# Routing a 64-expert layer: expert slots from eight rounds of max8 instead of ranks and one-hot matmuls, all gate/up products as split float32r passes, and the sum kept in two tensors

## The reference

```python
scores = sigmoid(t @ w_router)                  # 512 tokens x 64 experts, f32
sel = scores + b_router
# the best 4 of 8 groups (sum of each group's top 2), then the top 8 experts within them
w = scores at the 8 experts; w = w / w.sum() * 2.5
y = (silu(t @ w_sh_gate) * (t @ w_sh_up)) @ w_sh_down            # shared expert
y += sum over e: w[:, e] * ((silu(t @ w_gate[e]) * (t @ w_up[e])) @ w_down[e])
x = x + y
x = x + sigmoid(rms_norm(x) @ w_ple_gate) * rms_norm(p @ w_ple_proj)
```

## Time and profile before

| | |
|---|---|
| three runs | 1226.49, 1230.92, 1232.58 us (median 1230.92) |
| the profiled execution | 1230.64 us, of which 1228.9 us span |
| busy: PE, DVE, ACT, POOL | 1170.2, 811.1, 716.4, 311.3 us |
| expert loop, from the silu of expert 1 to that of 63 | 534.04 to 1152.29 us |
| mean granted clock of TensorE | 0.984 |

### The profile page before, as it was taken

One profiled execution on the slowest core, in us unless ns is written; L12 is line 12 of the kernel. 1 busy time (PEld: TensorE's weight loads), 2 busy tenths in 40 slices (PEclk: granted clock), 3 DMA queues, 4 the chain that ended last, 5 costly groups with the idle time before them and its releaser, 6 DMA issues. The chain is left out here.

```text
span 1228.9 us, 17964 instructions
## 1 busy us (share of the span) xinstructions
PE 1170.2 (95%) x5557; PEld 891.3 (73%) x5557; DVE 811.1 (66%) x1351; ACT 716.4 (58%) x1263; POOL 311.3 (25%) x291
## 2 busy tenths in 40 slices
PE   5999999998999999799999999999999999999778
PEld 5988888686566874377777777777777777777566
DVE  6336442387343426488888888888888888888642
ACT  5534442375343242277777777777777777777651
POOL 1210000051364000123233333333333333333200
PEclk9999999999899999899999999999999999999979
DMA  6313212024002068379999999999999999999641
GB/s 226 138 69 106 99 68 88 20 73 171 1 1 86 25 249 312 150 247 360 358 368 375 367 372 378 368 366 363 357 367 368 362 365 374 370 374 328 171 156 52
DMA packets 71756, 290.34 MB, mean 236 GB/s; under 512 B 15107, under 2 KB 20262, under 8 KB 46758
## 3 DMA queue, kind: packets, MB, share of 16 engines
q1 hardware_dynamic: 51846, 252.05, 53.2%
q0 software_dynamic: 19296, 35.71, 11.7%
q10 hardware_dynamic: 576, 2.10, 0.4%
HBM read 282.45 MB, written 41.94 MB: 264 GB/s over the span
## 5 line engine op out<-in xcount | busy, mean ns | idle before, releaser
L636 POOL DMA_INDIRECT moe_sum<-ya,sidx x64 | 132.1, 2064 | 397.7 <-DMA moe_sum<-ya,sidx 345.4
L1358 DVE TENSOR_TENSOR arena_r<-arena,win_r 128x1024 fp32r<-128x1024 f32 x192 | 223.2, 1218 | 0.5 <-ACT win_r L902 0.4
L902 ACT ACTIVATE win_r<-arena 128x1024 fp32r<-128x1024 f32 x192 | 191.3, 1094 | 10.7 <-PE bank L1657 10.7
L1738 PE MATMUL bank<-win_r,work_r 128*128 128x512 f32 x384 | 176.6, 460 | 0.0
L1376 DVE TENSOR_TENSOR arena_r<-arena,hT_r 128x1024 fp32r<-128x1024 f32 x128 | 151.2, 1222 | 29.7 <-ACT hT_r L921 29.7
L1740 PE MATMUL bank<-arena_r,work_r 128*128 128x512 f32 x384 | 150.0, 391 | 0.0
L1739 PE MATMUL bank<-win_r 128*128 128x512 f32 x384 | 149.7, 390 | 0.0
L921 ACT ACTIVATE hT_r<-arena 128x1024 fp32r<-128x1024 f32 x128 | 129.1, 1070 | 0.0
L1730 PE MATMUL bank<-arena,work 128*128 128x512 f32 x256 | 122.3, 601 | 1.6 <-ACT work L912 1.6
L1492 PE MATMUL bank<-arena_r,hT_r 128*128 128x512 f32 (+2 forms) x320 | 120.8, 378 | 0.1
L1496 PE MATMUL bank<-win_r,hT_r 128*128 128x512 f32 (+2 forms) x320 | 120.6, 377 | 0.0
(11 more groups left out here) (268 smaller groups left out, 2142.7 us busy)
## 6 DMA issues: line engine op xcount, KB each, us to landing
arena<-in_w_exp_gate SPq DMA_DIRECT2D x64, 1024.0 KB, 8.2
arena<-in_w_exp_up SPq DMA_DIRECT2D x64, 1024.0 KB, 11.6
arena<-in_w_exp_down SPq DMA_DIRECT2D x64, 1024.0 KB, 6.6
win<-in_w_in SPq DMA_DIRECT2D x8, 2048.0 KB, 7.8
win<-in_w_o SPq DMA_DIRECT2D x2, 2048.0 KB, 7.6
arena<-in_w_ple_gate SPq DMA_DIRECT2D x2, 2048.0 KB, 11.1
win<-in_mla_w_qb SPq DMA_DIRECT2D x4, 576.0 KB, 4.0
resid<-in_x SPq DMA_DIRECT2D x4, 512.0 KB, 5.0
```

Source lines behind the costliest of these rows:

```text
L636: pool.indirect_dma_start(sum_dram, bass.IndirectOffsetOnAxis(sidx[j % 2][0:NS, 0:1], 0), yo[j % 2][0:NS], None, bounds_check=last_token, ...
L902: act.activation(gu_hi[n % 2][:, :, cols], gu_w[n % RING][:, :, cols], ACT.Copy).then_inc(gu_hi_r, 1)
L1358: dve.tensor_tensor(gu_lo[n % RING][:, :, cols], gu_w[n % RING][:, :, cols], gu_hi[n % 2][:, :, cols].bitcast(F32), ALU.subtract).then_inc ...
L1738: pe.matmul(b_, x_hi[:, k, :], w_hi, start=False, stop=False)
```

## The change

- **Slots.** The key of a token for an expert is 4096 minus its number where the expert was chosen, else 0 (`rt_K`). PE transposes the keys once, so that 128 partitions hold 64 experts x two halves of the tokens, 256 keys each. Eight rounds of `max` (the 8 largest) and `match_replace` (strike them out) list the tokens of every half: 64 slots for each half of each expert (`tops_of`). Two copies and one matmul put the lists into slot order (`lists_of`, `slots_T`), and one instruction turns all keys into token numbers `idx`, 128 slots x 64 experts (`slot_tokens`). `one_hot`, `tab`, `tokens_of`, the ranks, the table `R` and `iota` go. An expert now fits in one pass if neither half of the tokens has more than 64 for it. In the last two steps of the loop the eight rounds run once more, for a next pass.
- **Weights.** The 64 combine weights of a token are stored behind its row, so a gathered row has 1088 instead of 1024 values. POOL copies column D + j of the gathered rows to `wt` for `hidden`, and column j of `idx` to the index tiles of gather and scatter: three copies of 128 x 1 for an expert.
- **Gate/up.** `KS` goes: all 8 blocks are split. There are four instead of three pieces of 128 x 1024 on ACT and on DVE, two instead of three copies of the transposed rows on ACT, and 24 split passes instead of 18 plus the 4 direct records.
- **Two sums.** Even experts are added to `sums[0]`, which starts as x (stored early), odd ones to `sums[1]`, which starts as the shared expert's output. A scatter waits only for the one two before it. After the loop both are loaded and DVE adds them (`add_odd`).
- **Shared expert.** Its steps are reordered: PE banks 0 to 3 for gate/up, and banks 6/7, 0/1, 2/3, 6/7 for the four outputs, copied (not added) by ACT for tiles 0 and 1 and by DVE for tiles 2 and 3. `sh_hidden(0)` stands behind the routing on DVE. Its weights use the other window buffer. The first half of the high parts of down now stands ahead of the silu on ACT. The zeroing of the gathered rows' buffers goes.

```diff
-        KS = 6
-        NPR = KS // 2
+        NPR = KD // 2
...
             def scatter(b, q, j):
-                pool.wait_ge(yA, at(b, q, 2, 2 * (j + 1)))
-                pool.wait_ge(yB, at(b, q, 1, j + 1))
                 if q is None and j == 0:
                     pool.wait_ge(sum_st, 16 * NT)
+                elif q is None and j == 1:
+                    pool.wait_ge(sum_odd_st, 16 * NT)
                 else:
-                    pool.wait_ge(scat[(j - 1) % 2], at(b, q, 8, 16 * ((j - 1) // 2 + 1)))
+                    pool.wait_ge(scat[j % 2], at(b, q, 8, 16 * (j // 2)))
                 pool.sem_inc(held, 1)
-                pool.indirect_dma_start(sum_dram, bass.IndirectOffsetOnAxis(sidx[j % 2][0:NS, 0:1], 0),
+                pool.tensor_copy(sidx[j % 2][:, :], tokens(q, j)).then_inc(sidx_set, 1)
+                pool.wait_ge(sidx_set, at(b, q, 1, j + 1))
...
+                pool.wait_ge(y_out, at(b, q, 2, 2 * (j + 1)))
+                pool.sem_inc(held, 1)
+                pool.indirect_dma_start(sums[j % 2], bass.IndirectOffsetOnAxis(sidx[j % 2][0:NS, 0:1], 0),
...
             def step(b, q, j):
                 if q is not None or 1 <= j <= E:
                     scatter(b, q, j - 1)
+                if q is not None or 0 <= j + 1 < E:
+                    weight(b, q, j + 1)
                 if q is not None or j + 3 < E:
                     gather(b, q, j + 3)
...
+            def tops_of(b, rounds):
+                for i in rounds:
+                    best = tops_[:, 8 * i:8 * i + 8]
+                    for c in range(2):
+                        ins = (dve.max(best, keys_) if c == 0 else
+                               dve.match_replace(out=keys_, in_to_replace=best, in_values=keys_, imm_value=0.0))
+                        ins.then_inc(tops_step, 1)
+                        n = 2 * i + c + 1
+                        dve.wait_ge(tops_step, n if b is None else at(b, None, 2 * ROUNDS / E, 2 * ROUNDS + n))
...
             def step(b, q, j):
                 free = q is None
-                if not free or j + 3 < E:
-                    select(b, q, j + 3)
...
                     b_ = bank[2 + j % 2][:, :]
-                    for k in range(KS, KD):
-                        pe.matmul(b_, x_f[:, k - KS, :], wgu[j % RING][:, k], start=(k == KS), stop=False)
                     pe.wait_ge(xt_hi, at(b, q, 2, 2 * j + 2))
-                    pe.wait_ge(xtb, at(b, q, 1, j + 1))
-                    for k in range(KS):
+                    pe.wait_ge(xt_lo, at(b, q, 1, j + 1))
+                    for k in range(KD):
...
+            sh_gate_up(0)
...
+            pe.wait_ge(K_ready, 1)
+            for c in range(2):
+                pe.transpose(KT[:, c * P:(c + 1) * P], rt_K[:, 2 * c:2 * c + 2, :].rearrange("q t e -> q (t e)"), ident[:, :])
...
+            sh_gate_up(1)
+            sh_gate_up(2)
+            slots_T(None)
+            sh_hidden_T(0)
+            sh_gate_up(3)
+            sh_hidden_T(1)
...
+            sh_down(0, 6)
+            sh_hidden_T(2)
+            sh_down(1, 0)
+            sh_hidden_T(3)
+            sh_down(2, 2)
+            pe.wait_ge(sh_y_act, 1)
+            sh_down(3, 6)
```

More of the change, by code:

```diff
@@ L82, in sem @@
             return ctx.enter_context(nc.semaphore(name))
+        bank = [ctx.enter_context(nc.psum_tensor(f"bank{i}", [P, 512], F32)) for i in range(8)]
         def v2(t, at, x, y):
@@ L211, in hybrid_block_kernel @@
         sidx = [sb(f"sidx{i}", 1, U32) for i in range(2)]
-        slots = [sm[:, 180 + 2 * i:182 + 2 * i] for i in range(4)]
-        wt = [z[:, 1:2] for z in slots]
+        wt = [sm[:, 180 + i:181 + i] for i in range(4)]
         rows = sb("rows", P)
@@ L249, in hybrid_block_kernel @@
         cmp_ = work[:, 964:964 + NPASS_MAX]
-        addt = sm[:, 176:180]
-        pcol = sm[:, 192:193]
-        bank = [ctx.enter_context(nc.psum_tensor(f"bank{i}", [P, 512], F32)) for i in range(8)]
+        kcol = sm[:, 176:180]
+        KT, counts, slot_keys = bank[5][:, 0:2 * P], bank[5][:, 2 * P:3 * P], bank[5][:, 0:E]
         ld_x = [sem(f"x_loaded{t}") for t in range(NT)]
@@ L443, in _ @@
             expert_dn(1, 1)
+            for t in range(NT):
+                sp.wait_ge(h2_n, t + 1)
+                sp.dma_start(sums[0][t * P:(t + 1) * P, :], x[:, t, :]).then_inc(sum_st, 16)
             for i in range(4):
@@ L1319, in first_selects @@
[L1319 to L1333 removed]
+                    last = dve.tensor_copy(x[:, m, half * 512:(half + 1) * 512], bank[b0 + half][:, :])
@@ L1359, in step @@
                                           gu_hi[n % 2][:, :, cols].bitcast(F32), ALU.subtract).then_inc(gu_lo_r, 1)
+                if free and j == -1:
+                    sh_out(NT - 1, 6)
+                if free and j == E - 1:
+                    tops_of(b, range(0, 4))
+                if free and j == E:
+                    tops_of(b, range(4, ROUNDS))
+                    lists_of()
                 if not free or 0 <= j < E:
@@ L1652, in hidden_T, with down @@
                 return last
-            def down(aT_buf, w):
+            def down(b0, aT_buf, w):
                 for half in range(2):
                     for k in range(KF):
-                        last = pe.matmul(bank[6 + half][:, :], aT_buf[:, k, :], w[:, k, half * 512:(half + 1) * 512],
+                        last = pe.matmul(bank[b0 + half][:, :], aT_buf[:, k, :], w[:, k, half * 512:(half + 1) * 512],
                                          start=(k == 0), stop=(k == KF - 1))
                 return last
-            def tab(b, j):
-                if b is None and j == 0:
-                    pe.wait_ge(R_ready, 1)
-                else:
-                    pe.wait_ge(idx_ready, ahead(b, j))
-                pe.wait_ge(sel_ready, ahead(b, j + 1))
-                for t in range(NT):
-                    last = pe.matmul(bank[5][:, 0:NC], S_[j % 2][:, t, :], Rv[:, j, t, :], start=(t == 0), stop=(t == NT - 1))
-                last.then_inc(tab_done, 1)
@@ L1712, in _, with slots_T, sh_gate_up, sh_hidden_T @@
-            pe.wait_ge(sh_y, NT)
+            def slots_T(b):
+                pe.wait_ge(lists_ready, 1 if b is None else at(b, None, 1 / E, 2))
+                pe.matmul(slot_keys, lists[:, :], pair[:, :], start=True, stop=True).then_inc(lists_T, 1)
+            def sh_gate_up(m):
+                pe.wait_ge(pj_free[m], P_PLE // 4 + 2)
+                gate_up(bank[m], hT[:, :, tok(m)], shgu).then_inc(sh_gu, 1)
+            def sh_hidden_T(m):
+                pe.wait_ge(sh_a, m + 1)
+                if m >= 1:
+                    pe.wait_ge(sh_aT, m)
+                hidden_T(a_[m % 2]).then_inc(sh_at, 1)
@@ new lines, in sh_down @@
+            def sh_down(m, b0):
+                pe.wait_ge(sh_aT, m + 1)
+                down(b0, aT[m], shdn).then_inc(sh_dn, 1)
+            sh_gate_up(0)
+            for i in range(2):
+                pe.wait_ge(tr_free[i], T_H3 // 2)
+            pe.wait_ge(K_ready, 1)
+            for c in range(2):
+                pe.transpose(KT[:, c * P:(c + 1) * P], rt_K[:, 2 * c:2 * c + 2, :].rearrange("q t e -> q (t e)"), ident[:, :])
+            for c in range(2):
+                last = pe.matmul(counts, ones[:, :], rt_M[:, 2 * c:2 * c + 2, :].rearrange("q t e -> q (t e)"),
+                                 start=(c == 0), stop=(c == 1))
```

427 lines of the change are left out of this document (184 added, 243 removed).

## The result

The changed kernel takes 1216.7 us (median of 4 runs, 1212.24 to 1219.14) against 1230.47 for the kernel before (median of 4, a fourth run added): ratio 0.989, 95% interval 0.985 to 0.993. It is faster, but by 14 us or 1.1%, where 40 us were forecast; 1191 and the whole range of 1177 to 1208 are missed. The profiled execution took 1215.48 us, its span 1213.7.

A forecast was written before the change was run, and what follows sets the result against it. The weights' DMA was to become the bound at 9.65 us a step: 528.1 + 59 x 9.65 + 14.3 = 1111.8, + 77.9 = 1189.7 us span, with 1.7 around it 1191.4; forecast 1191 us, range 1177 to 1208.

The forecast's parts named there:

- the DMA's time per step, 9.65 us: Expert loop: weights 7.49 us plus gather and scatter 2.06, low end 9.55, high end 9.86; 9.65 taken as the bound.
- the ring runs dry: Expert loop: the four weight buffers, full at the start, only delay the DMA bound; steps 9.3 us first, then 9.6 to 9.7.
- ACT never waited at 9.86, so the DMA has room: Expert loop: ACT had no wait for weights at 9.86 us a step, so 9.65 was taken, nearer the low end.
- PE's period of 9.3 us: Expert loop: PE's step falls from 9.86 us to 9.29, taken as 9.3, but is not reached because of DMA.
- The exchange: Gate/up on PE: 24 split passes, 5.47 us, replace the split and direct parts, 5.84 us, giving 0.37 us a step.
- POOL's waits "off the path": Expert loop: POOL waits 345.4 us for its own scatters, but nothing in the loop waited for a scatter.
- Before the loop: Shared expert and routing: keys at about 468, eight rounds of 8 us hidden, silu of expert 1 at 524.5, gaining 9.5 us.
- behind it: After the loop: from the silu of 63 to the end 77.9 us instead of 76.6, net +1.3.
- PE stays the bound: Rival, 25%: mixed packets cost DMA less, steps stay 9.3 to 9.4 us; run 1180.7 or 1186.9 us.
- The engines are really full: Rival, 13%: DMA engines have no time left, loop steps stay at 9.86 us; run 1203.7 us.
- POOL's copies hold up DVE: Rival, 9%: POOL's three copies block DVE's two-input subtractions, DVE needs 9.7 us a step; run 1205.5 us.
- Two scatters in flight hurt each other: Rival, 6%: overlapping scatters, or scatter beside weights, lengthen packets; slower than before (1237 us) at 10.42 us a step.

The follow-up runs named there:

- even15: Changed kernel with each half's filled slots dealt over all 16 DMA engines, the second half in opposite order: 1192.5 us, ratio 0.971.
- packed: Changed kernel with four ranks in a row placed on one DMA engine before the next is used: 1313.7 us, one run.
- the cleanest pair: even15_gfirst_noxlow, 1170.6 us, and the same omission and POOL order with the changed kernel's slots, 1207.8 us; one run each.
- even15_gfirst: even15 with POOL issuing weight copy and next gather first, the scatter last: 1183.3 us, ratio 0.962.
- even15_gfirst_noxlow: even15_gfirst with the rows' low parts left out of gate/up (DVE's subtraction, PE's pass), so less than the layer is computed: 1170.6 us, one run.
- even15_onewait: even15 with each scatter again waiting for the one before it, whichever sum it goes to: 1241.2 us, ratio 1.013.
- even15_onewait_gfirst: even15_onewait with POOL issuing the gather ahead of the scatter's wait: 1253.7 us, one run.
- even15_noxlow: even15 with the rows' low parts left out of gate/up, so less than the layer is computed: 1245.0 us, one run.

## Why the prediction was wrong, point by point

**The step that failed: the DMA's time per step, 9.65 us.** It was the sum of weights at 7.49 us and of gather and scatter at 2.06, both means over 16 engines, and its range ended at 9.86 because the loop before ran at that. It measured 10.09. What the sum lacked is that a load is as late as its slowest part, so that the fullest engine counts and not the mean; and the change moves rows there, 5.03 per expert instead of 4.47. That edit, the order in which slots are filled, was not costed at all. With even slots the same traffic needs 9.33 us, which is under the low end of 9.55: the mean was too high and the layout's price, 0.7 us, was missing.

That the ring runs dry after some twenty experts and the weights' loads become the bound came true, but by luck. The prediction had it from the mean, and by the mean as measured (9.33 us, level with PE's 9.36) the ring does not run dry: in even15 ACT waits for no weight. It ran dry in the changed kernel because of the slots, which the prediction left out. In the sum: the silu of 63 was forecast at 1111.8 and came at 1134.96. Of these 23.2 us, -1.6 lie before the loop and 24.8 in it; the tail adds 0.8.

That the placing of filled slots alone sets the time is shown by runs, and the traces show that some of the 16 parts of each load land late, in the number and by the degrees of the count. Which engine each part belongs to rests on the skill's map. Why the price of a row is not the same in both pairs (0.50 us from the changed kernel to packed, 0.70 for 0.98 rows in the cleanest pair) stays open, and so does why the mean share of busy time stays at 1.00 in the changed kernel while most parts are early.

**"ACT never waited at 9.86, so the DMA has room".** Right as far as it went: at 4.47 rows the kernel before didn't run dry. But its layout was taken over to the changed kernel unasked.

**PE's period of 9.3 us** was right: 9.36 us in even15_gfirst, PE full. The exchange gave 0.17 to 0.28 us of the 0.37.

**POOL's waits "off the path": wrong.** 345.4 us of waits for scatters with PE busy 95% looked harmless, and cost the kernel before 0.11 us a step. The prediction did see the 6.0 us of late gathers and that they would mostly go, but not that the chain of scatters is a period of its own. Put back into the changed kernel, the wait costs 34 us: the shorter the step becomes, the further it falls below a chain of scatters of 10 us and more. The two sums are thus worth more than the exchange, the other part that was undone, and the prediction gave them nothing in a DMA-bound loop.

**Before the loop** the keys (468), the rounds (8 us, to 478), the tokens and the silu of expert 1 (524.5, measured 522.9, in a spread of some 6 us) held; **behind it** 77.9 us, measured 78.7.

**The rivals.** *PE stays the bound* (25%) is what happens once slots are even: 1192.5 and 1183.3 us against its 1181 to 1187. *The engines are really full* at 9.86 erred to the right side, for a wrong reason: the share of busy time was 1.00 in the changed kernel too, and 395 GB/s were still to be had against 361 to 373. The rule cited there, loads from memory held to about 358 GB/s (the Trainium skill, "DMA: Bandwidth & Descriptors", Where 436 GB/s comes from), was held against all traffic in the prediction, and so put the step at 9.86 or above. Held against loads alone it gives an estimate of 9.6 us: 3.146 MB of weights and 4096/64 rows of 4352 B, 0.28 MB. The trace does not agree with it as a limit: in even15_gfirst_noxlow these loads take 9.33 us, 367 GB/s, beside the scatters. *POOL's copies hold up DVE*: no; DVE's subtraction of 128 x 1024 takes 296.5/256 = 1.16 us as before (215.1/185). It is the other way round: POOL's copy of the weight's column takes 0.7 to 1.8 us, and such copies lengthen the gather's way. In even15 the copies end at 807.52 and 808.68, within 0.1 us of the end of DVE's second and third subtraction (four of them fill 805.14 to 809.77); a copy beside another instruction takes 0.20.

```profile
805.75 1.77 POOL L625 COPY small<-ya 128x1 f32 x1
807.76 0.92 POOL L607 COPY gidx<-slot_tokens 128x1 uint32 x1 [0.23 <-issue]
...
810.71 0.20 POOL L641 COPY sidx<-slot_tokens 128x1 uint32 x1
```

```profile
805.14 4.63 DVE L1368 TENSOR_TENSOR arena_r<-arena,win_r 128x1024 fp32r<-128x1024 f32 x4 [0.52 <-ACT win_r L930]
```

*Two scatters in flight hurt each other*: no; keeping them apart is what costs.

**The best version** of these is even15_gfirst: the whole change, with even slots and the gather ahead of the scatter, 1183.3 us, 0.962 (0.959 to 0.965) of the kernel before and 33 us below the changed kernel. Its DMA (9.33) and its PE (9.36) are level.

## What to carry to other kernels

When rows are gathered or scattered over a partly filled tile, find out which partitions the filled ones are, and deal them out over all DMA engines: the time of every load that shares the engines goes by the fullest, and a mean share of 1.00 doesn't tell whether it is fair. How far apart the 16 parts of one load land does. Before an engine's wait is called harmless, compare the period of its chain (here scatter, landing, next scatter: 10 us) with the step that is aimed at, not with the present one. To measure one bound by taking work away, look first at what lies second: here it was a gather behind a scatter in one queue.

## What the runs showed of the hardware

- The same weights and rows moved at 390 to 395 GB/s with even slots (even15), at 361 to 373 in the changed kernel once its ring had run dry and at 306 to 334 with packed ones.
- The 16 parts of one load of 1024 KB landed within 3.7 us with even slots, 11.1 in the changed kernel and 15.4 with packed ones (medians).
- An accumulating scatter (64 rows on average, in 128 slots) landed 8.9 to 9.2 us after its issue in even15, where two are in flight, 7.3 to 8.6 in even15_onewait and 8.5 to 9.2 in even15_onewait_gfirst, where they never are; a gather took 7.8 to 8.0 in even15 (medians of windows of 40 us, beside the weights' loads).
- In even15_noxlow PE stood still for about 3 us in every second step, and the granted clock of its windows from 560 to 1040 us fell to 0.90 to 0.92; the window below, in which PE starts again at 811.90 after such a stop, has 0.63 on average, so most of it is at the lower of the two levels, 1.2 GHz; in even15_gfirst_noxlow, with as little work but waits of at most 2.1 us, it stayed at 0.98 to 1.00 there.

```profile
811.00:814.00 3.00, 2.10 (x9) 2.10 (x10) 2.47 (x3) 0.42 (x3) 1.87 (x2) 0.63 1.01 332
```
